# Expert weights of a diffusion step in 2 MB pieces with 16 KB runs instead of 1 MB pieces with 8 KB runs

## The reference

```python
def expert_choice_ffn(h, p):
    n = B * L
    cap = CAPACITY_FACTOR * n // N_EXPERTS
    xs = h.reshape(n, D)
    aff = jax.nn.softmax((xs @ p['w_router']).astype(jnp.float32), axis=-1)
    g, idx = lax.top_k(aff.T, cap)
    xe = xs[idx]
    a = jnp.einsum('ecd,edf->ecf', xe, p['w_exp_gate'])
    u = jnp.einsum('ecd,edf->ecf', xe, p['w_exp_up'])
    ye = jnp.einsum('ecf,efd->ecd', jax.nn.silu(a) * u, p['w_exp_down']) * g[..., None].astype(h.dtype)
    out = jnp.zeros((n, D), h.dtype).at[idx.reshape(-1)].add(ye.reshape(-1, D))
```

## Time and profile before

| | us |
|---|---|
| runs (three) | 2621.17, 2626.64, 2627.45 |
| the profiled execution's own time | 2621.07 |
| its span | 2619.3 |
| TensorE busy | 2410.7 (92%) |
| VectorE busy | 508.1 (19%) |
| ScalarE busy | 234.5 (9%) |
| mean granted clock of TensorE | 0.97 of full |

### The profile page before, as it was taken

The page is one execution under the profiler, slowest core; times in us unless marked ns, Lnnn a source line. Parts: engine busy times, 40 slices in busy tenths (PEclk is TensorE's granted clock), DMA queues, the critical chain, the costliest instruction groups (busy, mean ns, idle before and its releaser), DMA issues.

```text
span 2619.3 us, 22817 instructions
## 1 busy us (share of the span) xinstructions
PE 2410.7 (92%) x9040; PEld 1120.4 (43%) x9040; DVE 508.1 (19%) x1025; ACT 234.5 (9%) x478; POOL 44.2 (2%) x54
## 2 busy tenths in 40 slices
PE   5899999999999999999999977988888888888886
PEld 2355554444466666555554434322222222222222
DVE  4301111323122111000001114111111211111125
ACT  1100001000021111000000012100000000000001
POOL 0000000000000000000000000000000000000000
PEclk8999999999999999999999998999999999999998
DMA  9964553444412223454433220899999999999995
GB/s 361 352 232 160 190 192 133 174 159 164 160 65 97 89 72 135 139 193 129 153 104 130 96 96 0 370 421 421 422 422 421 422 421 422 422 422 422 422 421 218
DMA packets 196641, 644.73 MB, mean 246 GB/s; under 512 B 8423, under 2 KB 57992, under 8 KB 147112
## 3 DMA queue, kind: packets, MB, share of 16 engines
q1 hardware_dynamic: 194312, 635.55, 62.4%
q10 hardware_dynamic: 2208, 8.24, 0.8%
q0 software_dynamic: 64, 0.13, 0.0%
HBM read 640.21 MB, written 3.67 MB: 246 GB/s over the span
## 4 chain that ended last, share of the span: by engine, by line
PE 75%; DMA 19%; DVE 2%; ACT 1%; issue 1%; SPq 1%; DVEq 1%; POOL 0%; ACTq 0%; POOLq 0%
PE PS L407 16%; DMA ring<-in_w_up 16%; PE PS L640 12%; PE PS L392 10%; PE PS L840 9%; PE PS L675 6%; PE PS L795 6%; PE PS L659 3%; PE PS L366 3%; DMA ring<-in_w_ada 2%; PE PS L765 2%; PE PS L740 1%; DVE RG L1566 1%; DMA ring<-in_w_in 1%; PE PS L630 1%
## 5 line engine op out<-in xcount | busy, mean ns | idle before, releaser
L795 PE MATMUL PS<-ring,RF 128*48 128x512 f32 x1920 | 435.7, 596 | 79.2 <-DMA ring<-in_w_up 77.2
L640 PE MATMUL PS<-RB,ring 128*128 128x384 f32 x1024 | 335.9, 486 | 0.0
L795 PEld LDWEIGHTS PS<-ring,RF 128*48 128x48 f32 x1920 | 135.4, 123 | 374.1 <-issue 373.6
L1561 DVE TENSOR_TENSOR RC<-RC,PS 128x512 f32<-128x512 f32 x192 | 122.5, 683 | 736.5 <-PE PS L765 736.5
L640 PEld LDWEIGHTS PS<-RB,ring 128*128 128x128 f32 x1024 | 194.2, 190 | 138.0 <-issue 3.4
L392 PE MATMUL PS<-RB,ring 128*128 128x384 f32 x768 | 251.0, 489 | 2.1 <-DMA ring<-in_w_in 2.1
L407 PE MATMUL PS<-ring,RB 128*128 128x512 f32 x576 | 252.4, 593 | 0.0
L840 PE MATMUL PS<-ring,RF 128*48 128x512 f32 x960 | 231.9, 645 | 0.0
L392 PEld LDWEIGHTS PS<-RB,ring 128*128 128x128 f32 x768 | 146.2, 191 | 108.9 <-issue 9.5
L407 PE MATMUL PS<-ring,RC 128*128 128x512 f32 x384 | 165.7, 592 | 0.6 <-DVE RC L1417 0.6
L407 PEld LDWEIGHTS PS<-ring,RB 128*128 128x128 f32 x576 | 108.1, 190 | 132.1 <-issue 131.8
(11 more groups left out here) (223 smaller groups left out, 1283.6 us busy)
## 6 DMA issues: line engine op xcount, KB each, us to landing
ring<-in_w_gate SPq DMA_DIRECT2D x128, 1024.0 KB, 12.0
ring<-in_w_up SPq DMA_DIRECT2D x128, 1024.0 KB, 13.8
ring<-in_w_down SPq DMA_DIRECT2D x128, 1024.0 KB, 13.5
ring<-in_w_ada SPq DMA_DIRECT2D x48, 2048.0 KB, 14.0
ring<-in_w_in SPq DMA_DIRECT2D x40, 2048.0 KB, 8.0
ring<-in_w_attn_o SPq DMA_DIRECT2D x8, 2048.0 KB, 15.8
ring<-in_w_out SPq DMA_DIRECT2D x8, 2048.0 KB, 8.2
ring<-in_w_hy_o SPq DMA_DIRECT2D x4, 2048.0 KB, 8.0
```

The costliest lines, as they stand in the source:

```text
L640: last = mm(bank(F0, T), wide[:, n % 4, k, t % 2 * P:(t % 2 + 1) * P], hT[:, k, :], start=k == 0, stop=k == KT - 1)
L795: last = mm(bank(n, p0=64 * u, p1=64 * u + SLOTS), xeT[:, kk, 0, :] if first else x_cur[:, kk, :], pieces[:, (2 * i + u) % 8, k * FF + n * ...
L1561: tt(facc[:, m, q], facc[:, m, q], bank(4 + n % 4), ALU.add).then_inc(e_acc, 1)
```

## The change

The ring becomes four pieces of 2 MB. A gate or up piece holds 512 rows, four in each partition (a run of 16 KB); a down piece holds 256 rows, two in each partition (16 KB). There are 12 pieces and 9 releases per expert instead of 24 and 21. TensorE waits for a pair of 4 MB and makes 32 records before it gives it back; `beside` comes after each pair. A down piece is given back after two row blocks. In the last expert two transfers of 1 MB with runs of 4 KB fill a piece, on one semaphore. The channels' order changes from pairs to fours (`fourfold`) in all places named above; the columns of `h_s` are read by twos, where they were contiguous, because two rows of down now share a partition; the router's weights come in four transfers instead of two.

```diff
-PIECES, RELEASES = 24, 21
+PIECES, RELEASES = 12, 9
-def paired(k):
-    return slice(2 * P * (k // 2) + k % 2, 2 * P * (k // 2 + 1), 2)
+def fourfold(k):
+    return slice(4 * P * (k // 4) + k % 4, 4 * P * (k // 4 + 1), 4)
-        pieces = view(ring_t, 0, 8, 2 * FF)
+        ring4 = view(ring_t, 0, 4, 4 * FF)
...
-                return w[ds(e * D + i * 2 * P, 2 * P), :].rearrange("(p k) n -> p (k n)", k=2)
-            def down_piece(e, k):
-                return w_down[ds(e * FF + k * P, P), :]
+                return w[ds(e * D + i * 4 * P, 4 * P), :].rearrange("(p k) n -> p (k n)", k=4)
+            def down_piece(e, c):
+                return w_down[ds(e * FF + c * 2 * P, 2 * P), :].rearrange("(p k) n -> p (k n)", k=2)
...
                 for q in range(PIECES):
-                    if first and q < 8:
-                        sp.wait_ge(blocks_used, N_EX - 4 + (q // 2 + 1))
-                    elif q < 7:
-                        sp.wait_ge(piece_used, e * RELEASES + (q - 6))
-                    elif q == 7:
+                    if first and q < 4:
+                        sp.wait_ge(blocks_used, N_EX - 3 + q)
+                    elif q < 3:
+                        sp.wait_ge(piece_used, e * RELEASES + (q - 2))
+                    elif q == 3:
                         sp.wait_ge(down_done, e * 2)
-                    elif q < 22:
-                        sp.wait_ge(piece_used, e * RELEASES + (q - q % 2 - 6))
+                    elif q < 10:
+                        sp.wait_ge(piece_used, e * RELEASES + (q - q % 2 - 2))
                     else:
                         sp.wait_ge(gu_done, e * 2 + 2)
...
                     elif final:
-                        sp.dma_start(slot.rearrange("p (k n) -> p k n", k=2),
-                                     down_half(e, (q - 16) // 4, (q - 16) % 4 * 2)).then_inc(piece_in[q % 8], 16)
+                        for c in range(2):
+                            sp.dma_start(piece(q)[:, 2 * c * FF:2 * (c + 1) * FF].rearrange("p (k n) -> p k n", k=2),
+                                         down_half(e, (q - 8) // 2, (q - 8) % 2 * 2 + c)).then_inc(piece_in[q % 4], 16)
...
-                for i in range(KT // 2):
+                for i in range(KT // 4):
                     landing(2 * i)
                     landing(2 * i + 1)
-                    for k in range(2):
-                        kk = 2 * i + k
+                    for k in range(4):
+                        kk = 4 * i + k
...
-                    if i < KT // 2 - 1:
+                    if i < KT // 4 - 1:
                         last.then_inc(piece_used, 2)
-                    if i % 2 == 1:
-                        beside(i // 2)
+                    beside(i)
...
-                        o, src, i_ = bank(2 + n, SLOTS, j * SLOTS), h_s[0:SLOTS, n, j * P:(j + 1) * P], \
+                        o, src, i_ = bank(2 + n, SLOTS, j * SLOTS), h_s[0:SLOTS, n, j // 2 * 2 * P + j % 2:(j // 2 + 1) * 2 * P:2], \
...
                 for k in range(HK):
-                    landing(16 + k)
+                    c, j = k // 2, k % 2
+                    if j == 0:
+                        landing(8 + c)
...
-                    if k < HK - 1:
+                    if j == 1 and c < 3:
                         last.then_inc(piece_used, 1)
...
-            for j in range(2):
-                pool.dma_start(wr.rearrange("p (c j) e -> p c j e", j=2)[:, :, j, 0:NE],
-                               w_router.rearrange("(c p j) e -> p c j e", p=P, j=2)[:, :, j, :]).then_inc(wr_in, 16)
+            for j in range(4):
+                pool.dma_start(wr.rearrange("p (c j) e -> p c j e", j=4)[:, :, j, 0:NE],
+                               w_router.rearrange("(c p j) e -> p c j e", p=P, j=4)[:, :, j, :]).then_inc(wr_in, 16)
...
-                                  .rearrange("x (h p j) -> x h j p", h=2, j=2),
-                                  bank(b0 + n % 2).rearrange("x (h j p) -> x h j p", h=2, j=2)).then_inc(used, 1)
+                                  .rearrange("x (p j) -> x j p", j=4),
+                                  bank(b0 + n % 2).rearrange("x (j p) -> x j p", j=4)).then_inc(used, 1)
```

More of the change, by code:

```diff
@@ L201, in build @@
         gate_read, mixed = sem("gate_read"), sem("mixed")
-        piece_in = [sem(f"piece_in{j}") for j in range(8)]
+        piece_in = [sem(f"piece_in{j}") for j in range(4)]
         piece_used, gu_done, down_done = sem("piece_used"), sem("gu_done"), sem("down_done")
@@ L325, in expert @@
                         sp.wait_ge(down_done, e * 2)
-                    elif q < 22:
-                        sp.wait_ge(piece_used, e * RELEASES + (q - q % 2 - 6))
+                    elif q < 10:
+                        sp.wait_ge(piece_used, e * RELEASES + (q - q % 2 - 2))
                     else:
                         sp.wait_ge(gu_done, e * 2 + 2)
[L330 to L333, removed]
+                    if q < 8:
+                        sp.dma_start(piece(q), gate_piece(w_up if q % 2 else w_gate, e, q // 2))\
+                            .then_inc(piece_in[q % 4], 16)
@@ L337, in expert @@
                     else:
-                        sp.dma_start(slot, down_piece(e, q - 16)).then_inc(piece_in[q % 8], 16)
+                        sp.dma_start(piece(q), down_piece(e, q - 8)).then_inc(piece_in[q % 4], 16)
             expert(0, first=True)
@@ L776, in beside, with landing @@
                         broadcast_gates(2 * t, 2, ones2, diag2_ready, g2_bc, g2_used)
-                def landing(q):
-                    pe.wait_ge(piece_in[q % 8], e * 48 + 16 * (q // 8 + 1))
+                def landing(q, more=0):
+                    pe.wait_ge(piece_in[q % 4], e * 48 + 16 * (q // 4 + 1) + more)
                 if not first:
@@ L796, in expert @@
                                           xeT[:, kk, 0, :] if first else x_cur[:, kk, :],
[L797 removed]
+                                          piece(2 * i + u)[:, k * FF + n * NC_:k * FF + (n + 1) * NC_],
                                           start=kk == 0, stop=kk == KT - 1)
@@ L818, in expert @@
                     for i in range(2):
-                        for q in range(4):
-                            landing(16 + 4 * i + q)
-                            if i == 0 and q == 2:
+                        for q in range(2):
+                            landing(8 + 2 * i + q, 16)
+                            if i == 0 and q == 1:
                                 pe.wait_ge(e_hT, e * 2 + 2)
-                            if i == 1 and q == 2:
+                            if i == 1 and q == 1:
                                 pe.wait_ge(sc_st, NE)
@@ L827, in expert @@
                                     scatter(NE, 0, m, m)
-                            for k in range(2):
+                            for k in range(4):
                                 for u in range(2):
-                                    last = mm(bank(2 + i, p0=64 * u, p1=64 * u + SLOTS), hTe[:, 2 * q + k, :],
-                                              pieces[:, 4 * i + q, k * FF + u * NC_:k * FF + (u + 1) * NC_],
-                                              start=q == 0 and k == 0, stop=q == 3 and k == 1)
+                                    last = mm(bank(2 + i, p0=64 * u, p1=64 * u + SLOTS), hTe[:, 4 * q + k, :],
+                                              piece(8 + 2 * i + q)[:, k * FF + u * NC_:k * FF + (u + 1) * NC_],
+                                              start=q == 0 and k == 0, stop=q == 1 and k == 3)
                         last.then_inc(down_done, 1)
```

26 lines of the change are left out of this document (14 added, 12 removed).

## The result

| | before | after |
|---|---|---|
| median of the runs, us | 2623.90 (2620.21 to 2627.45, 4 runs) | 2729.89 (2722.45 to 2734.04, 4 runs) |
| span of the profiled execution, us | 2619.3 | 2726.1 |
| first product of expert 0, us | 1639.92 | 1652.74 |
| expert 0 | 52.0 | 62.3 |
| mean period, experts 1 to 14 | 59.81 | 65.26 |

The ratio is 1.0406, 95% interval 1.0388 to 1.0424: slower, as forecast (2650), but by 106 us instead of 23, outside the range. The rows of the table add up: 12.8 + 10.3 + 14 x 5.45 + 7.4 = 106.8 us, the difference of the spans.

The account below looks back on a forecast made before the run. Expert part taken as bound by transfers (422 GB/s). Start +3.1, periods +11.8, end of expert 14 +3.4 +0.9 -0.2, strides +4.3 gave +23 us on 2621.07: 2644; median 5.6 above, so 2650, range 2614 to 2678.

Parts of the forecast that it names:

- The rate: Expert weight stream: 16 KB runs give 428.7 GB/s, 58.7 us an expert against 59.66.
- Rival D: Expert weight stream: a 16 KB run moves like two of 8 KB, no rate gain; 2659 us, chance 0.10.
- Does the stream stand still?: Experts' ring: slack 0.5 us in gate/up, so no loss at full clock; late only at the next expert's turn.
- the turn: Next expert's first refill, after down's first quarter: late by 1.8 us per expert; period 60.5, +11.8 us over 14.
- L: Landing of an expert's last gate/up piece, from which the times at the turn are counted.
- the end of expert 14: After expert 14's last landing: +3.4 us gate/up work, +0.9 chain and down, -0.2 wait before the last expert.
- Rival A: Gate/up: merged waits pull the clock down there too, 15 to 33 us more, 2665 to 2683; chance 0.20.
- Rival B: Turn between experts: slots back in time, no gap, -13.4 us in place of +11.8; 2625 us, chance 0.30.
- The start and the strides: Expert 0's stream resumes later, +3.1 us; strided loads +4.3 together (L375 0.8, L707 2, L813 1.5).
- rival C: Strided weight loads: stride 4 doubles them, 35 us in place of 4.3, +31; 2681 us, chance 0.05.
- The last expert: Last expert: TensorE sets the end, refills are covered beside broadcasts, cost nothing; uncovered, 1 to 2 us a pair.
- The small edits on POOL and SyncE: Two more router DMAs on POOL, half as many SyncE issues: cost nothing, a few us at most if uncovered.

Follow-up runs that it names:

- e17: Changed kernel, gate piece before up, each released by itself; SiLUs beside the last up products; ScalarE writes modulation rows in the order of fours: 2611.31 us, 0.9951.
- e19: Changed kernel with channels in pairs and 8 KB runs, gate piece before up, SiLUs beside the last up products: 2618.44 us, 0.9991.
- e3: Changed kernel with extra products on TensorE, not part of the computation, so that it idles less: 2712.88 us, 1.0348.
- e14: Kernel before, 1 MB transfers, with both landing waits and releases only by fours of pieces (twos in down): 2700.21 us, 1.0295.
- e2: Changed kernel with the old order of channels: four 2 MB pieces, each as two 8 KB runs in a partition: 2709.37 us, 1.0343.
- e15: Changed kernel; TensorE goes through the gate piece, then the up piece, each waited for and given back by itself: 2627.59 us, 1.0019.
- e5: Changed kernel; ScalarE writes the modulation's rows already in the order of fours, so L381's weight loads are contiguous: 2716.89 us, 1.0374.
- e1: Kernel before with the order of fours and its strides; ring, 1 MB pieces and 8 KB runs as before: 2637.45 us, 1.0070.
- e10: Kernel before with slots given back by fours (twos in down), landings waited for as before: 2627.44 us, 1.0022.
- e12: Kernel before with landings waited for by fours (twos in down), slots given back as before: 2645.57 us, 1.0090.

## Why the prediction was right in sign and wrong in size

**The rate: right.** 428.7 GB/s and 58.7 us an expert were forecast from a fixed 9.7 ns per run. e17 shows 428 to 429 and periods of 58.7 to 58.8 in most experts (mean 59.03, with 62.2 for expert 14). Rival D is out by e19. (The lower bound with the fixed part gone is 601.8 ns a run and 57.8 us, not 600.9 and 57.7; nothing hangs on it.) The fabric's ceiling of 435 GB/s that the Trainium skill gives (DMA: Bandwidth & Descriptors, Specifications) was not reached in any window shown here.

**"Does the stream stand still?": the step that failed.** The prediction gave the pair in gate/up a slack of 0.5 us, 19.1 against 19.6, "so no loss at full clock". The term that was mis-sized is the 2.2 us between issue and landing. It was read from the first 1 MB piece into a queue that had stood idle and applied to the landing of a whole group in the running loop, where the group ahead is still landing when the next is issued (for another 0.7 us in the kernel after, 2.4 in e3). There the rows have 3.2 us (13.0 less 9.78, after) and 4.2 us (14.0 less 9.78, e3). With them the round is 7.07 + 0.18 + 13.0 + 0.1 = 20.4 to 21.4 us: the slack is -0.8 to -1.8, and the rounds measured are 21.45 (e3) and, with a block at the low clock, 22.1 us (after). The size of the transfer explains little of it: e14's groups of 1 MB transfers add 3.0 to 4.2 us as well, and into an idle queue a 2 MB piece adds 2.7 us with 8 KB runs (7.7 us to land, e2) and 3.3 with 16 KB runs (after). So the loss fell where the prediction had excluded it, in gate/up, besides the turn that it had named. The turn itself was timed well: the first refill comes 18.9 us after the last pair's start at 2008.92 less 0.1 (forecast L + 7.05 + 12.13 = L + 19.2). But the same term is short there too: the piece landed 9.2 us after its issue, where 2.2 + 4.89 = 7.09 stood. The sum had +11.8 for the periods, +4.1 at the end of expert 14 and 1.5 for L813: 17.4 in all; they were 76.3.

**Rival A had the follow-up, not the cause.** It said that merged waits would pull the clock down in gate/up. They did: after waits of 4.13 and 4.21 us the blocks took 8.77 and 8.45 in place of 7.07. But e3 kept the clock at 0.97 and regained 15 us of 106, and in e15 the clock's losses there vanish with the holes. Rival A's own price, 15 to 33 us, was about right for the clock's share (15 by e3; the slower matmuls of expert 5, 2.1 us, would be 29 over 14 experts); the holes under it were missing.

**Rival B was out, for a reason that can be undone.** It needed the slots back in time. Nothing in the transfers forbade that: e15 gives the gate piece back 3.5 us earlier, and its mean period is 58.90, near B's 58.7.

**The start and the strides: too small.** Expert 0's first product came 12.8 us later, where 0.8 + 2 stood for L375 and L707. "6 ns, if another doubling costs as much again" carried the step from stride 1 to 2 on to 4; measured are 190, 196 and 329 ns, not a law of doublings. The 12.8 us are of two single executions: six kernels with the order of fours and L381's strided loads start expert 0 at 1648.30 to 1652.74, eight with the old order at 1637.90 to 1640.79, and the means are 11.0 us apart. By e5 and e17 the L381 loads are 8.7 to 9.0 us of it, to within some 4 us of such scatter. This is rival C's mechanism in one place: the Trainium skill's rule (SBUF — State Buffer, Specifications), at least two hits in a 16-byte line, agrees in direction with 329 against 196 ns; its price on L707 did not come (231 against 214), so C's 31 us didn't either. The gathers' loads rose too, from 197 ns in the median (L737, L740) to 308 and 326 (L743, L746), and stayed hidden behind the wider products but for some 0.03 us a round, as forecast. Expert 0 itself was 10.3 us longer, forecast 3.1: its refills meet the same negative slack (51.8 in e15, with the same strides).

**The last expert: "nothing" was +7.4.** It begins with a block at the low clock (8.77, after a wait of 2.74), its broadcasts' first products take 3.44 us in place of 1.98, the copies of the gate rows, at 1067 ns, are waited for 1.32 us where 0.78 was, and the first 48 down products take 12.24 us, not 10.51. By e1 (95.4 us) some 5 us come with the order of fours, by e2 (95.5, old order) as many with the coarse ring; the two don't add to more than 7.4. With gate first, the order of fours is what is left: 93.3 us in e17, 89.3 in e19. TensorE's timeline of the last expert, after:

```profile
2628.72 8.77 PE L801 MATMUL PS<-ring,RF 128*48 128x512 f32 x32 [2.74 <-DMA ring<-in_w_up]
...
2640.71 3.44 PE L696 MATMUL PS<-RF,RE 128*128 128x512 f32 x4 [2.15 <-DVE RF L1450]
...
2676.13 1.13 PE L771 MATMUL PS<-RG,RF 48*128 48x512 f32 x4 [1.32 <-DVE RE L1461]
...
2681.09 12.24 PE L835 MATMUL PS<-ring,RF 128*48 128x512 f32 x48
```

**The small edits on POOL and SyncE cost nothing that shows**, as said: e17, which keeps them all and the slower gate copies too, starts expert 0 at 1639.34, before at 1639.92.

**Open.** Why the way from issue to landing is 2.2 to 3.3 us longer than the transfer at an idle queue and 3.0 to 4.2 in the loop was not tried. In e3 the queue never stops at the hole but moves 246 GB/s from 1983 to 1986, while the pair before is still landing, which would fit DMA engines that are out of step, some without work before the last one is through; the runs don't part that from a fixed delay. How far 2 MB transfers add to the grain is bounded only: e2 less e14 is 9 us by the medians, 13 by the ratios.

## What to carry to other kernels

Before a prefetch ring is made coarser, add up one slot's round (work on the piece, issue, issue to landing of the whole group that is waited for) and compare it with the ring's pure transfer time; a slack of half a microsecond that rests on a delay read at an idle queue is none. Give back and wait for the smallest unit that the loop order allows: reordering the products so that one tensor's piece is finished before the next was worth 101 us here, with the same products and transfers. And look for the cost of a new stride at each line that reads or writes with it: writing the rows in the right order on an engine with time to spare took 9 us off.

## What the runs showed of the hardware that was not expected

- Prices of waits don't add: 6 and 24 us alone, 79 together (e10, e12, e14), which fits one slack that both draw on.
- A weight load of 128x128 in 4-byte elements takes 190 ns contiguous, 196 with stride 2 and 329 with stride 4 (the gathers' loads 197 and then 308 to 326); the loads of single-pass transposes take 141, 214 and 231 (L754, L707, L713). A VectorE copy of 128x512 that writes in the order of fours takes 1067 ns against 691 in the old order.
- Into an idle queue a 2 MB transfer in 16 KB runs lands 8.2 us after its issue, 3.3 us more than it moves bytes. In the running loop a group of 4 MB takes 12.9 to 14.1 us for 9.8 to 9.9 us of transfer, whether it is two transfers of 2 MB or four of 1 MB (after, e3, e14); the group ahead was still landing when these were issued, so a part of it is that group's rest.
- A fixed 9.7 ns per run, read from 2, 4 and 8 KB, held at 16 KB: 428.7 GB/s worked out, 428 to 429 measured.
